# 22 row chunks with both activation parts as one 512-column operand, and a block inverse that starts from the identity

## The reference

```
# mixer of the first model, first branch
a_b, a_c, a_v = ...                         # u @ w_in, 1024 columns each
y_a = (a_b * causal_dwconv(a_c * a_v, conv_w)) @ w_out_a      # 3 taps

# cross attention of the first model
q = u @ w_q ;  k, v = split(mem_n @ w_kv)
o = softmax(q k^T / 16) v

# memory keys of the second model
mem_k = mem_n @ w_mem_kv[:, :256]

# gated delta rule, per head and chunk of 64 tokens
lower = where(strict, (kb k^T) * decay, 0)
sol   = triangular_solve(I + lower, rhs, unit_diagonal=True)
```

## Time and profile before

| what | value |
|---|---|
| median of three runs | 1541.56 us |
| the profiled execution's own time | 1541.43 us |
| its span | 1539.6 us |
| PE busy | 1509.3 us, 98% of the span |
| POOL busy | 1155.9 us, 75% |
| ACT busy | 830.3 us, 54% |
| DVE busy | 605.1 us, 39% |
| chain that ended last, by engine | PE 83%, DVE 9%, ACT 4% |

### The profile page before, as it was taken

The page is one execution under the profiler, slowest core; times in us unless marked ns, Lnnn a source line. Parts: engine busy times, 40 slices in busy tenths (PEclk is TensorE's granted clock), DMA queues, the critical chain, the costliest instruction groups (busy, mean ns, idle before and its releaser), DMA issues.

```text
span 1539.6 us, 22902 instructions
## 1 busy us (share of the span) xinstructions
PE 1509.3 (98%) x9276; PEld 1307.5 (85%) x9276; DVE 605.1 (39%) x1008; ACT 830.3 (54%) x1293; POOL 1155.9 (75%) x499
## 2 busy tenths in 40 slices
PE   9999999999999999999999999999999999999997
PEld 7888889999878898888888898888888888888886
DVE  3111016447786712331330498772113747311101
ACT  6444364375756536364554687155445476564443
POOL 8888978888758888578869796317888963388893
PEclk9999999999999999999999999999999999999999
DMA  6555555565644555265555563105555542355552
GB/s 232 191 189 192 181 191 180 175 212 181 211 152 141 199 181 193 91 209 187 186 184 194 171 211 124 44 29 196 178 186 200 194 160 75 106 176 184 191 196 78
DMA packets 71865, 259.87 MB, mean 169 GB/s; under 512 B 7984, under 2 KB 8784, under 8 KB 71504
## 3 DMA queue, kind: packets, MB, share of 16 engines
q1 hardware_dynamic: 69552, 250.97, 49.4%
q10 hardware_dynamic: 2208, 7.43, 1.3%
HBM read 257.29 MB, written 1.08 MB: 168 GB/s over the span
## 4 chain that ended last, share of the span: by engine, by line
PE 83%; DVE 9%; ACT 4%; issue 2%; POOL 1%; DMA 1%; ACTq 0%; DVEq 0%; POOLq 0%
PE bank L537 14%; PE bank L539 14%; PE bank L538 13%; PE bank L567 5%; PE bank L569 5%; PE bank L568 5%; PE bank L507 5%; PE bank L509 5%; PE bank L508 5%; PE bank L681 1%; ACT w_hi L1352 1%; DVE dec L2231 1%; DVE dec L2234 1%; PE bank L653 1%; DVE sq_mem L2059 1%
## 5 line engine op out<-in xcount | busy, mean ns | idle before, releaser
L440 POOL TENSOR_TENSOR w_lo<-raw,w_hi 128x1024 fp32r<-128x1024 f32 x468 | 1129.0, 2445 | 337.6 <-ACT w_hi L1352 337.1
L1352 ACT ACTIVATE w_hi<-raw 128x1024 fp32r<-128x1024 f32 x474 | 487.9, 1058 | 286.1 <-DMA raw<-in_w 281.8
L537 PE MATMUL bank<-w_hi,u_hi 128*128 128x512 f32 x872 | 345.8, 397 | 2.4 <-POOL w_lo L464 2.0
L539 PE MATMUL bank<-w_hi,u_lo 128*128 128x512 f32 x872 | 340.9, 391 | 0.0
L538 PE MATMUL bank<-w_lo,u_hi 128*128 128x512 f32 x872 | 340.3, 390 | 0.0
L507 PE MATMUL bank<-u_hi,w_hi 128*128 128x256 f32 x688 | 196.7, 286 | 0.0
L537 PEld LDWEIGHTS bank<-w_hi,u_hi 128*128 128x128 f32 x872 | 164.3, 188 | 36.5 <-POOL w_lo L464 2.2
L509 PE MATMUL bank<-u_hi,w_lo 128*128 128x256 f32 x688 | 194.7, 283 | 0.0
L508 PE MATMUL bank<-u_lo,w_hi 128*128 128x256 f32 x688 | 194.6, 283 | 0.0
L539 PEld LDWEIGHTS bank<-w_hi,u_lo 128*128 128x128 f32 x872 | 164.0, 188 | 35.0
L538 PEld LDWEIGHTS bank<-w_lo,u_hi 128*128 128x128 f32 x872 | 164.4, 188 | 32.6
(11 more groups left out here) (432 smaller groups left out, 2072.0 us busy)
## 6 DMA issues: line engine op xcount, KB each, us to landing
raw<-in_w SPq DMA_DIRECT2D x474, 512.0 KB, 4.4
bc<-acs_scratch ACTq DMA_DIRECT2D x8, 512.0 KB, 4.6
mem_t<-in_mem ACTq DMA_DIRECT2D x2, 1024.0 KB, 6.3
xf<-in_x SPq DMA_DIRECT2D x2, 512.0 KB, 7.0
out<-out_t SPq DMA_DIRECT2D x4, 256.0 KB, 2.7
lvl<-in_lvl ACTq DMA_DIRECT2D x1, 448.0 KB, 3.0
band<-in_band ACTq DMA_DIRECT2D x1, 256.0 KB, 6.1
tri<-in_tri SPq DMA_DIRECT2D x1, 192.0 KB, 8.0
```

The costliest lines, as they stand in the source:

```text
L440: nc.gpsimd.tensor_tensor(w_lo[:, q % RAW, :], raw[:, q % RAW, :], w_hi[:, q % HI, :].bitcast(F32), ALU.subtract).then_inc(split_done, 1)
L537: mm(b[:], hi[:, kt, a], w_hi[:, q % HI:q % HI + 2, c], start=kt == 0, stop=False, skip_group_check=True)
L539: m = mm(b[:], lo[:, kt, a], w_hi[:, q % HI:q % HI + 2, c], start=False, stop=kt == KT - 1, skip_group_check=True)
L1352: fn(w_hi[:, q % HI, :], raw[:, q % RAW, :], ACT.Copy).then_inc(hi_made, 1)
```

## The change

**Wide chunks.** High and low activations lie interleaved in one array (`u_both`, likewise for the memory arrays). In `short_cv`, `short_b`, `mem_k`, `xq` and `mem2k`, 22 chunks in all, `wide_stage` takes the place of `row_stage`: `w_hi` is multiplied by both parts at once (512 columns), `w_lo` by the high part (256 columns), so 32 matmuls a chunk instead of 48. High and low results lie in two halves of a bank; a chunk has two tiles and so takes two banks, where it took one. DVE adds the halves with two TENSOR_REDUCE (`summed`). ACT's `ctmp` copy is gone: DVE sums both chunks of a pair, the second into bank 4, and multiplies them.

```diff
+WIDE = ('short_cv', 'short_b', 'mem_k', 'xq', 'mem2k')
+def banks_of(r):
+    name, j = STAGE_OF[r], r - G0[STAGE_OF[r]]
+    if name in WIDE:
+        return [2 * r % 4, 2 * r % 4 + 1]
...
+def freed_for(r, b):
+    return max([e + 1 for e in range(r) if b in banks_of(e)], default=0)
...
+            def wide_stage(name, both, ready=None, sub=None):
+                j0, n = sub or (0, NUM[name])
+                for j in range(j0, j0 + n):
+                    r = G0[name] + j
+                    for h in range(2):
+                        q = P0[name] + 2 * j + h
+                        pe.wait_ge(split_done, q + 1)
+                        for t in range(2):
+                            b = tile_bank(r, t)
+                            if h == 0 and freed_for(r, banks_of(r)[t]):
+                                pe.wait_ge(row_free, freed_for(r, banks_of(r)[t]))
+                            for k in range(4):
...
+                                mm(b[:], w_hi[:, q % HI, a], both[:, kt, :, :], start=kt == 0, stop=False, skip_group_check=True)
+                                m = mm(b[:, 0, :], w_lo[:, q % RAW, a], both[:, kt, 0, :], start=False, stop=kt == KT - 1, skip_group_check=True)
+                        m.then_inc(piece_done, 1)
...
-                act.wait_ge(piece_done, a + 2)
...
-                fn(ctmp[j % 2][:], bank[g % 4][:], ACT.Copy).then_inc(W["short_act"], 1)
...
+            def summed(stage, j, out):
+                for t in range(2):
+                    m = v.tensor_reduce(out[:, t, :], tile_bank(G0[stage] + j, t)[:].rearrange("p a c -> p c a"), AX.X, ALU.add)
+                m.then_inc(row_free, 1)
...
+                dve.wait_ge(piece_done, P0["short_cv"] + 4 * j + 2)
+                summed("short_cv", 2 * j, ctmp[j % 2])
                 dve.wait_ge(piece_done, P0["short_cv"] + 4 * j + 4)
+                summed("short_cv", 2 * j + 1, sum_bank("short_cv"))
+                dve.wait_ge(row_free, g + 2)
+                v.tensor_tensor(cv[:, 2 * j:2 * j + 2, :], ctmp[j % 2][:], sum_bank("short_cv")[:], ALU.mult).then_inc(W["short_act"], 1)
...
-                v.tensor_tensor(cc[:, a, :], cc[:, a, :], bank[(G0["short_b"] + j) % 4][:], ALU.mult).then_inc(row_free, 1)
+                summed("short_b", j, sum_bank("short_b"))
+                dve.wait_ge(row_free, G0["short_b"] + j + 1)
+                v.tensor_tensor(cc[:, a, :], cc[:, a, :], sum_bank("short_b")[:], ALU.mult).then_inc(W["row_done"], 1)
```

```diff
-LEVELS = [2, 4, 8, 16, 32, 64]
+LEVELS = [1, 2, 4, 8, 16, 32, 64]
...
-            for n in range(3):
-                if n == 1:
-                    gate(1, 1)
-                b = start_unit(U0["x0"] + n)
-                pe.wait_ge(W["lev_e"], 4 if n else 2)
...
+                                m = mm(b[a, 0, o], lt[a, k % 6, c:c + 64], iX[a, k, :] if li else ident[a, a], start=True, stop=True)
                     m.then_inc(unit_done, 1)
+                if li == 0:
+                    gate(1, 1)
...
-                    v.tensor_tensor(iE[a, 6 * c:6 * c + 6, :], lt[a, :, 256 * c + p0:256 * c + p0 + 64],
-                                    lvl[a, 0:1, a].to_broadcast([64, 6, 64]), ALU.mult).then_inc(W["lev_e"], 1)
...
-            v.tensor_tensor(iY, eye[:].unsqueeze(1).to_broadcast([P, GS, 64]), iE[:], ALU.subtract).then_inc(W["lev_x"], 1)
...
+                        now = iYX[:, :, a, :] if li else eye[:].unsqueeze(1).unsqueeze(1).to_broadcast([P, 2, 4, 64])
+                        v.tensor_tensor(iYX[:, :, a, :], now, b, ALU.subtract).then_inc(unit_free, 1)
+            memory_max(2)
+            memory_max(3)
```

More of the change, by code:

```diff
@@ L149 @@
 SPL = {n: i for i, n in enumerate(["ffn0", "mix", "xattn", "ffn1", "mix_a", "ffn2", "kv", "mix_b", "ffn3"])}
+WIDE = ('short_cv', 'short_b', 'mem_k', 'xq', 'mem2k')
+STAGE_OF = [name for name, n, kind in ORDER if kind not in ("acc", "proj") for _ in range(n)]
+def banks_of(r):
+    name, j = STAGE_OF[r], r - G0[STAGE_OF[r]]
+    if name in WIDE:
+        return [2 * r % 4, 2 * r % 4 + 1]
+    if name.startswith("ffn"):
+        return [2 - j % 3]
+    if name in ("mq1", "q1") and r < G0["q1"] + 3:
+        return [(G0["mq1"] + (r - G0["mq1"]) % 2) % 4]
+    return [4] if (name, j) == ("gz", 2) else [r % 4]
+def freed_for(r, b):
+    return max([e + 1 for e in range(r) if b in banks_of(e)], default=0)
+DONE0 = {"short_b": 0, "xbc": 4, "qkv": 16}
 S0 = {}
@@ L351, in row_bank, with tile_bank, sum_bank @@
             return bank[r % 4]
+        def tile_bank(r, t):
+            return bank[banks_of(r)[t]]
+        def sum_bank(stage):
+            return bank_of(U0["bacols"] + 2) if stage == "qkv" else bank[4]
         score_banks = [bank[G0["kv_v"] % 4], bank[G0["kv_k"] % 4], bank[4]]
@@ L380, in tail_unit, with memory_bank @@
             return U0["tail"] + TAIL.index(name)
+        def memory_bank(i):
+            return bank[(3, 4, 3, 0)[i]]
         def o_bank(n):
@@ L815, in _ @@
             pair_stage("gate_a", u_hi, u_lo, sub=[(1, 0), (1, 1)])
-            row_stage("short_cv", u_hi, u_lo)
-            row_stage("short_b", u_hi, u_lo)
+            wide_stage("short_cv", u_both)
+            wide_stage("short_b", u_both)
             pair_stage("short_out", h_hi, h_lo, lambda s, kt: pe.wait_ge(W["short_lo"], kt // 2 + 1))
@@ L1062, in _ @@
             pe.wait_ge(W["loaded_lvl"], 16)
-            for i in range(5):
+            for i in range(6):
                 for p0 in (0, 64):
                     a = slice(p0, p0 + 64)
-                    m = mm(b[a, 0, 64 * i:64 * i + 64] if i < 4 else b[a, 1, 0:64], lvl[a, i + 1, a], ident[a, a], start=True, stop=True)
+                    m = mm(flat(b)[a, 64 * i:64 * i + 64], lvl[a, i, a], ident[a, a], start=True, stop=True)
             m.then_inc(unit_done, 1)
@@ L1674, in _ @@
             after(q0 + 8)
-            mem_root(0, rs, bank[(G0["mem_k"] + 3) % 4])
+            mem_root(0, rs, tile_bank(G0["mem_k"] + 1, 1))
             after(q0 + 10)
@@ L1782, in memory_exp @@
                 for c in range(2):
-                    m = fn(pr_m[i][:, c, :], bank[3 + i % 2][:, c, :], ACT.Exp, bias=stat(1, i)[:, c:c + 1], scale=0.125,
+                    m = fn(pr_m[i][:, c, :], memory_bank(i)[:, c, :], ACT.Exp, bias=stat(1, i)[:, c:c + 1], scale=0.125,
                            accum_out=stat(2, i)[:, c:c + 1])
@@ L1990, in ffn, with sum_rows @@
                 hid_lo(f, 10)
+            def summed(stage, j, out):
+                for t in range(2):
+                    m = v.tensor_reduce(out[:, t, :], tile_bank(G0[stage] + j, t)[:].rearrange("p a c -> p c a"), AX.X, ALU.add)
+                m.then_inc(row_free, 1)
+            def sum_rows(stage, dst, j0=0, n=None):
+                for j in range(j0, n if n is not None else NUM[stage]):
+                    dve.wait_ge(piece_done, done(stage, j + 1))
+                    summed(stage, j, dst(j))
             def copy_rows(stage, dst, j0=0, n=None):
@@ L2381, in _ @@
             rstd("mix_a", 1)
[L2382 removed]
+            sum_rows("mem2k", lambda j: mk[j][:])
             lo_part("mix_a", 0, "ln_mix_a")
```

119 lines of the change are left out of this document (50 added, 69 removed).

## The result

The changed kernel takes 1553.60 us (median of 4 runs, 1551.54 to 1554.16) against 1541.43 for the kernel before (median of 4): a ratio of 1.0081 with an interval of 1.0069 to 1.0093, so 12 us slower, with the interval from 10.6 to 14.3. The forecast was 1545.0 with a range up to 1550.5. The sign was right, the size was not, and the time lies outside the range.

What follows compares the result with a forecast made beforehand. PE, busy 98% of the span, was taken to bound the kernel. Short convolution +8.3, mem_k, xq and mem2k −0.1, inverse −4.6 gave +3.6 us on 1541.43, so 1545.0 us, range 1536.5 to 1550.5.

Steps and rivals of the forecast that it cites:

- mem2k: Stage mem2k: −0.4 us on PE, but the transposes behind wait for ACT's xn, so 0 net.
- The short convolution: short_cv and short_b to short_out: PE savings, waits for banks and lost clock sum to +8.3 us (+2 to +13).
- The first wait: PE waits ahead of the fifth short_cv chunk for banks freed by sums behind the taps: 5.6 us (4.3 to 7).
- the second: PE's wait for chunk 8's banks in the convolution's third round: 4 us or none, taken as 2.
- the one ahead of `short_out`: short_out needs the bank of the last short_b chunk, which must be summed first: 1.7 us, none before.
- the low clock: In the convolution, reduced granted clock after PE's 5.6 us idle: 1.5 us lost (0 to 3, with two waits).
- Rival 1: Short convolution: six taps under 7.5 us also in the first round, only short_out's wait remains; 1536 us, chance 0.15.
- rival 3: Short convolution: one wait only, third round fast and clock holds; 1541.5 us, no change, chance 0.20.
- rival 2: Short convolution: taps one per POOL operation, every round late, waits of 7 and 5, clock lost twice; 1551 us, chance 0.14.
- The inverse: From gate(1, 0) to the last level: less PE idle and low clock, −4.6 us (−3 to −5.7).
- The wide step: Inner-dimension step of wide chunks on PE: 0.347 us instead of 0.360, 13 ns less, 0.21 us a chunk.
- Rival 4: Wide chunks on PE: fusing saves nothing, the 4.6 us of all wide chunks do not come; 1549.5 us, chance 0.03.

Runs made afterwards that it cites:

- The experiment alone: Only the inverse part of the change, all 22 chunks back to row chunks with their old evictions: 1537.68 us against 1541.41 before, ratio 0.9982.
- the kernel with all waits taken away: Changed kernel with taps reading PSUM, mem2k's sums ahead of the reciprocal, banks of short_out and xq turned: 1533.98 us, ratio 0.9967 to the kernel before.

## Why the prediction was wrong

**mem2k: the step that failed.** The prediction said "`mem2k`: −0.4 on PE, but the transposes behind it wait for ACT's `xn` ... So 0". I looked at what stands right behind the two chunks, and not at who needs their banks next. `mem2v` does, and its first bank comes free with a sum that stands on DVE behind a reciprocal which waits for ACT. The same copies stood there before, just as late, but `mem2v` had two other banks. It cost 3.1 us of idle time and 2.4 of low clock, 5.4 in the profile and 6.0 by the experiment. For `short_cv`, `short_out` and `xq` I had asked the question; here it was left out. No rival held it either. With these sums alone moved forward the kernel takes 1547.59, inside the range.

**The short convolution: right in mechanism, too small in size.** The first wait was forecast at 5.6 (4.3 to 7) and is 7.2: the taps went by one per POOL operation, at 2.5 us each, 15.0 in all, past even the upper end (14.3), where I took a middle. The experiment with taps from PSUM shows the cause. By the distance between starts the first wait costs 7.3, the second 1.4 where I took 2, the one ahead of `short_out` 1.6 where I took 1.7, the low clock 1.7 where I took 1.5. Four chunks take 5.65 instead of 5.55, 0.4 more. Together −2.5 + 7.3 + 1.4 + 1.6 + 1.7 + 0.4 = +9.9 for +8.3. Rival 1 (fast taps) and rival 3 (one wait, no clock lost) fall; of rival 2 the first wait came and the second was 1.1 instead of 5: PE's first wait had left POOL idle for 8.39 us, as the prediction's point against it said. The Trainium skill ("SBUF — State Buffer", section Who interferes with whom) says that a VectorE instruction with at most one SBUF input, outside its two-port modes, does not contend with GpSimd; the trace agrees, with 0.45 us a tap from PSUM against 2.5. The two TENSOR_SCALAR in SBUF have one such input as well and took 2.5; whether they ran in a two-port mode no trace here shows.

**The inverse: right**, in size and in its parts: −3.5 up to level 2's second set (forecast −3.7), −1.2 from there to the last level's end (−0.9), full clock, no idle time. The experiment alone gives −3.7 by the medians.

**The wide step: right only behind a break.** The prediction took 0.347 us, 13 ns less than before, for a stream in which nothing waits. In the changed kernel most chunks of the convolution run so, but all of those stand behind a wait; the first four take 0.353, and in the kernel with all waits taken away all twelve do (67.83 us for 192 steps). So where nothing waits a step is 7 ns cheaper, and a chunk saves 0.11 and not 0.21 us. That is a term mis-sized by half, small beside the waits. By the prediction's own sign, a step that is not 13 ns cheaper, it fails there. Rival 4 falls: twelve such chunks without waits still gain 1.3. The 2.5 ns that the Trainium skill ("TensorE: Matmul & The Clock Gate", section Back-to-back issue gap) gives for an isolated matmul would by estimate make 0.04 us a chunk; 0.11 to 0.21 was measured.

**The range** took in the unknown sizes of the known waits only. All steps but `mem2k` together, as the profile has them, make 1541.4 + 10.3 − 5.4 = 1546.3, or 1547.9 with the clock alike at the start of the program; the experiment gave 1547.59.

## What to carry to other kernels

When a stage takes twice the banks, go through every stage that follows one: who writes these banks next, what frees them, and what stands ahead of that on its engine. An eviction that was late and harmless becomes a wait as soon as its bank is needed. A DVE operation that works in SBUF beside a busy GpSimd can be five times as slow as one that reads PSUM, so what frees a bank should not stand behind it; keeping the operand in PSUM cost a bank here, and 0.44 instead of 0.31 us for a TENSOR_SCALAR when POOL rests (0.45 either way for the others).

## What was not expected of the hardware

The same alternation of 512 and 256 columns ran at two paces at full clock: 5.65 us a chunk when it followed the stage ahead of it without a pause (through all twelve chunks in the kernel with taps from PSUM), 5.55 after PE had waited for 0.8 us or more. Why is open. The same holds in `xq`: 5.55 behind a wait of 0.83 in the changed kernel, 5.65 without one in the kernel with all waits taken away. A wait is not the only way: in `mem_k` of that kernel half a chunk takes 2.82 ahead of eight transposes and 2.77 behind them, with no wait between. And in `kv_v`, behind two idle gaps of 1.0 us, the granted clock fell to between 0.60 and 0.65 in five of the ten profiles and stayed full in the other five, worth some 1.4 us each time. Behind the idle time of 2.0 to 2.4 us near the start of the program it fell to between 0.64 and 0.67 in five of the ten (not the same five). What decides it was not tried. A difference of 1 to 2 us between two single profiles can therefore be this alone.
